# A hybrid decoder layer on one core: mixing and memory attention of tokens 0 to 511 placed among the sparse attention units of tiles 4 to 7, and the wide counts over four tiles

## The reference

```python
proj = h @ w_in[l] + b_in[l]
dq, dk, dv, iq, ik, iw, sq, sk, sv = split(proj)          # rotary on dq, dk, iq, ik, sq, sk
o_dsa = dsa_sparse_attention(dq, dk, dv, iq, ik, iw)      # 8 heads, one shared K/V head
o_swa = swa_sink_attention(sq, sk, sv, swa_sinks[l])      # 8 heads, 2 K/V heads, window 128
mix = concatenate([o_dsa, o_swa], axis=-1) @ w_o[l]
h = layer_norm(DEEPNORM_ALPHA * h + mix, ln1_g[l], ln1_b[l])
c = memory_cross_attention(h, mem, wq_mem[l], wk_mem[l], wv_mem[l], wo_mem[l])   # 4 heads, 256 tokens
h = layer_norm(DEEPNORM_ALPHA * h + c, ln2_g[l], ln2_b[l])
m = square(relu(h @ w_up[l])) @ w_down[l]
h = layer_norm(DEEPNORM_ALPHA * h + m, ln3_g[l], ln3_b[l])
```

## Time and profile before

| | |
|---|---|
| median of three runs | 1640.76 us |
| profiled execution | 1633.94 us, span 1632.1 us |
| PE busy | 1513.5 us, 93% |
| PE weight load busy | 1286.1 us, 79% |
| DVE busy | 892.2 us, 55% |
| ACT busy | 465.4 us, 29% |
| POOL busy | 536.1 us, 33% |
| chain that ended last, by engine | PE 77%, DVE 14%, ACT 3%, issue 3% |

### The profile page before, as it was taken

The page is one execution under the profiler, slowest core; times in us unless marked ns, Lnnn a source line. Parts: engine busy times, 40 slices in busy tenths (PEclk is TensorE's granted clock), DMA queues, the critical chain, the costliest instruction groups (busy, mean ns, idle before and its releaser), DMA issues.

```text
span 1632.1 us, 20732 instructions
## 1 busy us (share of the span) xinstructions
PE 1513.5 (93%) x7720; PEld 1286.1 (79%) x7720; DVE 892.2 (55%) x1819; ACT 465.4 (29%) x987; POOL 536.1 (33%) x540
## 2 busy tenths in 40 slices
PE   7999975888768999989999999999999999999996
PEld 6887754888757998768887788888888888888884
DVE  7568986778877433593426733333333333333357
ACT  3014435788674651122211201111101011111010
POOL 5232214665510003341233153333333333333300
PEclk9999997999887999999999999999999999999998
DMA  6564223554410004211110221111111110111001
GB/s 224 178 190 149 94 100 127 179 173 151 141 46 16 12 7 168 97 42 49 52 53 0 78 78 52 52 52 52 52 52 52 52 52 29 49 52 52 1 26 78
DMA packets 61331, 128.96 MB, mean 79 GB/s; under 512 B 6960, under 2 KB 34096, under 8 KB 53552
## 3 DMA queue, kind: packets, MB, share of 16 engines
q1 hardware_dynamic: 44208, 100.37, 18.6%
q10 hardware_dynamic: 17024, 27.27, 4.7%
HBM read 100.35 MB, written 27.26 MB: 78 GB/s over the span
## 4 chain that ended last, share of the span: by engine, by line
PE 77%; DVE 14%; ACT 3%; issue 3%; POOL 1%; DMA 1%; ACTq 0%; SPq 0%; DVEq 0%; POOLq 0%
PE banks L651 22%; PE banks L653 22%; PE banks L652 22%; PE banks L844 3%; PE banks L703 2%; PE banks L704 2%; DVE unread L1483 2%; PE banks L831 2%; ACT unread_wide L1047 2%; PE banks L853 1%; DVE h_buf L1792 1%; DVE bn L1778 1%; PE banks L800 1%; DVE trial L1460 1%; DVE h_buf L1801 1%
## 5 line engine op out<-in xcount | busy, mean ns | idle before, releaser
L637 POOL TENSOR_SCALAR w_hi<-raw 128x512 fp32r<-128x512 f32 x268 | 174.5, 677 | 1011.9 <-PE banks L653 685.0
L642 POOL TENSOR_TENSOR w_lo<-raw,w_hi 128x512 fp32r<-128x512 f32 x268 | 363.9, 1389 | 0.0
L1892 DVE TENSOR_TENSOR h_buf<-h_buf,banks 128x1024 f32<-128x1024 f32 x112 | 136.7, 1221 | 145.8 <-PE banks L653 145.8
L651 PE MATMUL banks<-act_hi,w_hi 128*128 128x512 f32 x512 | 200.0, 391 | 1.7 <-DVE act_lo L1771 1.7
L651 PE MATMUL banks<-w_hi,hid_hi 128*128 128x512 f32 x512 | 199.3, 389 | 1.4 <-DVE hid_lo L1872 1.4
L653 PE MATMUL banks<-act_hi,w_lo 128*128 128x512 f32 x512 | 199.9, 390 | 0.0
L652 PE MATMUL banks<-act_lo,w_hi 128*128 128x512 f32 x512 | 199.7, 390 | 0.0
L653 PE MATMUL banks<-w_hi,hid_lo 128*128 128x512 f32 x512 | 199.2, 389 | 0.0
L652 PE MATMUL banks<-w_lo,hid_hi 128*128 128x512 f32 x512 | 199.2, 389 | 0.0
L1263 ACT ACTIVATE relu_buf<-banks 128x512 f32<-128x512 f32 x64 | 38.3, 599 | 523.4 <-PE banks L653 523.4
L1867 DVE TENSOR_TENSOR relu_buf<-relu_buf 128x512 f32<-128x512 f32 x64 | 45.0, 704 | 241.9 <-ACT relu_buf L1263 241.9
(11 more groups left out here) (178 smaller groups left out, 2779.6 us busy)
## 6 DMA issues: line engine op xcount, KB each, us to landing
raw<-w_up_dram SPq DMA_DIRECT2D x16, 1024.0 KB, 4.8
raw<-w_down_dram SPq DMA_DIRECT2D x16, 1024.0 KB, 4.8
q_tile<-qk_dram SPq DMA_DIRECT2D x176, 64.0 KB, 2.1
qk_dram<-q_hi ACTq DMA_DIRECT2D x28, 256.0 KB, 2.2
qk_dram<-roped ACTq DMA_DIRECT2D x28, 256.0 KB, 2.6
x_raw<-x_t_dram SPq DMA_DIRECT2D x8, 512.0 KB, 8.4
raw<-wk_mem_dram SPq DMA_DIRECT2D x4, 1024.0 KB, 5.4
raw<-wv_mem_dram SPq DMA_DIRECT2D x4, 1024.0 KB, 5.2
```

The costliest lines, as they stand in the source:

```text
L637: pool.tensor_scalar(w_hi[s][:, col], raw[r % 2][:, col], 1.0, 1.0, ALU.mult, ALU.mult)\
L642: pool.tensor_tensor(w_lo[s][:, col], raw[r % 2][:, col], w_hi[s][:, col].bitcast(F32), ALU.subtract).then_inc(w_ready, 1)
L651: pe.matmul(dst, lh, rh, start=(first and n == 0), stop=False)
L1892: dve.tensor_tensor(h_buf[:, t, :], h_buf[:, t, :], ring_l[n % 2][:], ALU.add)\
```

## The change

- Tokens are cut into two groups of four tiles. The three stages of products are run per group: group 0 (tiles 0 to 3) with 24 products placed inside the loop of sparse units, group 1 (tiles 4 to 7) after it. `step_of_product` gives the places, counted from the first sparse step: products 0 and 1 at steps 9 and 13, then 2 to 23 at steps 19, 20, 22, 24, 26, 28, 29, 31, 33, 35, 37, 38, 40, 42, 44, 46, 47, 49, 51, 53, 54, 54. Four empty steps (`GAP`) stand between the units of tile 3 and those of tile 4.
- The 12 chunks of these stages are loaded and split twice, once for each group. Those of group 0 use slots 0 and 1 only; from `C_LATE` on four slots rotate.
- Tile 4 becomes the fourth wide tile. ACT counts 31 bits over tiles 7, 6, 5 and 4: six beside the halves 22 to 27, 21 in the band's steps 3 to 38, four at steps 1, 6, 11 and 16 of the sparse units. Each tile's trial has its own semaphore step.
- The indexer's scores move to halves 10 and 11 (tiles 2, 3) and 15 to 18 (tiles 7, 6, 5, 4). The score of each tile is prepared for the search by itself (`prepare`) in place of one block over six tiles.
- From unit 7 on POOL and not DVE makes the low parts of the rotated tiles, between its weight chunks.
- The memory tokens have a buffer of their own; they are loaded after the last index score, and split before the last half is rotated, whose rotation moves to step 2 of the band. Memory products start at step 2.

```diff
-C_G = C_MIX + 4
-C_U = C_G + 4
-C_MLP = C_U + 4
+GROUP = 4
+C_LATE = C_MIX + 12
+C_MLP = C_LATE + 12
...
+INDEX_HALVES = {10: 2, 11: 3, 15: 7, 16: 6, 17: 5, 18: 4}
+PREPARE_HALVES = {12: 2, 13: 3, 19: 7, 20: 6, 21: 5, 22: 4}
...
+WIDE_HALF = 22
+NARROW_HALVES = (13, 14)
+POOL_SPLIT = 7
...
+def unit_at(n):
+
+    d = n - NS
+    if d >= 2 * HEADS:
+        d = d - GAP if d >= 2 * HEADS + GAP else -1
+    return d if d < ND else -1
+
+
+def step_of_product(g):
+
+    if g < 2:
+        return NS + HEADS + 1 + 4 * g
+    return min(NS + 2 * HEADS + 3 + 18 * (g - 2) // 10, N_STEPS + 2)
...
+def turned_at(grp, g):
+
+    out = [(0, GROUP * grp + g + grp + 1)] if g + grp + 1 < GROUP else []
+    for gg, k in ((grp, g), (grp - 1, N_GEMM + g)):
+        if gg == grp or (grp == 1 and g < 2):
+            stage, t = divmod(k - GROUP - 2, 2 * GROUP)
+            if 0 <= stage < 3 and 0 <= t < GROUP:
+                out.append((stage + 1, GROUP * gg + t))
+    return out
...
-WIDE = N_SEL - 3
+WIDE = N_SEL - 4
...
+COUNT_TICKS = [("step", 3 + 37 * j // N_STEP_BITS) for j in range(N_STEP_BITS)]
+COUNT_TICKS += [("step", NS + n) for n in (1, 6, 11, 16)] + [("product", g) for g in range(2, WIDE_LEFT - N_STEP_BITS - 2)]
...
-    for n in range(12):
-        stage, ch = divmod(n // 2, 2)
-        last[C_MIX + n] = ("L", L_GEMM + 16 * stage + 8 * ch + NT - 1)
+    for n in range(24):
+        grp, pair = divmod(n // 2, 6)
+        last[C_MIX + n] = ("L", L_PROD[grp, GROUP * pair + GROUP - 1])
...
         def slot_of(c):
-            return c % 2 if c < C_MIX else (c - C_MIX) % 4
+            return c % 2 if c < C_LATE else (c - C_LATE + 2) % 4
...
-                if 2 <= c < C_MIX + 2:
+                if 2 <= c < C_LATE:
                     chunk_used(pool, c - 2)
-                elif C_MIX + 2 <= c < C_MIX + 4:
+                elif C_LATE <= c < C_LATE + 2:
 
                     attended(pool, 2 * NT - 1)
-                elif c >= C_MIX + 4:
+                    chunk_used(pool, C_MIX + 9)
+                elif c >= C_LATE + 2:
                     chunk_used(pool, c - 4)
...
+                for g in products_of_step(n):
+                    for key in first_turned(0) if g == 0 else ():
+                        turn(*key)
+                    product(0, g)
+            for key in first_turned(1):
+                turn(*key)
             for g in range(N_GEMM):
-                product(g)
-                if g + 2 < NT:
-                    turn_o(g + 2)
-                if transposed_at(g):
-                    turn_result(*transposed_at(g))
+                product(1, g)
...
+            for v in range(last_half):
+                if v in PREPARE_HALVES:
+                    prepare(PREPARE_HALVES[v] - FIRST_TOPK_TILE)
+                if v in NARROW_HALVES:
+                    select_for(BUDGET_BAND)
+                if wide_bit_beside_rope(v) is not None:
+
+                    pending.extend(set_wide(wide_bit_beside_rope(v)))
+                    flush(0 if v % 2 else 2)
+                rotate_and_split(v)
+                flush()
+            split_mem()
+            pending.extend(set_wide(wide_bit_beside_rope(last_half)))
+
+            for n in range(N_STEPS + 4):
...
```

More of the change, by code:

```diff
@@ L895, in product @@
                 mm.then_inc(l_full[n % 2], 1)
+                for stage, t in turned_at(grp, g):
+                    turn(stage, t)
             def up(u):
@@ L1258, in rectify @@
+            load_x(1, 0)
+            load_x(1, 1)
+            for key in first_turned(1):
+                round_turned(*key)
+            for g in range(N_GEMM):
+                gemm(1, g)
             def rectify(q):
@@ L1536, in bisect @@
                     narrow_set(*waiting)
-                def bisect_alone(c, beside):
-                    for k in range(top, -1, -1):
-                        cost, counted = narrow_tally(c)
-                        yield cost + 0.3, None
-                        more = next(beside, None)
-                        if more is not None:
-                            yield more
-                        narrow_set(c, k, counted)
-                    yield from beside
                 def finish_narrow(cols):
@@ new lines, in gemm @@
+                    if stage != 1 and ch == 1:
+                        emptied(dve, l_free, n)
+                        moments(ln_at(stage // 2, t), t)
+                turned = turned_at(grp, g) if g < N_GEMM else []
+                for key in turned:
+                    if key[0] == 0:
+                        low_turned(*key)
+                if g:
+                    stage, ch, t = parts_of_product(grp, g - 1)
+                    if stage == 1:
+                        mem_probs(grp, g - 1)
+                    elif ch == 1:
+                        norm(ln_at(stage // 2, t), t)
@@ L1864, in square @@
+            for key in first_turned(1):
+                low_turned(*key)
+            norm(ln_at(1, GROUP - 1), GROUP - 1)
+            for g in range(N_GEMM + 1):
+                gemm(1, g)
+            for g in (N_GEMM, N_GEMM + 1):
+                for key in turned_at(1, g):
+                    low_turned(*key)
             def square(q):
```

819 lines of the change are left out of this document (448 added, 371 removed).

## The result

| | kernel before | changed kernel |
|---|---|---|
| median of four runs | 1641.2 us | 1743.8 us (1735.6 to 1746.3) |
| ratio, 95% interval | | 1.061 (1.058 to 1.065) |
| span of the profiled execution | 1632.1 us | 1744.2 us |
| PE busy | 1513.5 us, 93% | 1556.5 us, 89% |
| DVE / ACT / POOL busy | 892 / 465 / 536 us | 890 / 504 / 661 us |

The change costs 102.6 us by the medians, where 41.7 were forecast.

The account below looks back on a forecast made before the run. TensorE, busy 93% of the span, was taken as the bound. The terms moved the last product from 912.4 to 954.1 us; that +41.7 on the median 1640.8 gave 1682 us, range 1640 to 1718.

Parts of the forecast that it names:

- Projections and start of the band: Up to the first memory product: projection gaps go, -7.4 us; earlier memory product, -18; less half clock there, -2.
- Band, +9 for the fourth tile: Band steps: counting tile 4 on ACT and its fourth trial on DVE add 9 us, bounds 0 and +18.
- Units 0 to 15 and the last count: Early sparse part: units, counts and products 0 and 1 end at 493.8 us; 13.5 more until product 3 at 507.3.
- Weights, +51.8: Group 0's interleaved products: with two slots, PE waits at five pair changes for POOL's rounding, 51.8 us in sum.
- Turns behind LayerNorm, +13: Interleaved part: units' transposes wait for banks DVE frees after LayerNorm, at six products, 13 us, bounds 0 and 25.
- Clock, +8: Interleaved part: half clock after five weight stalls, 2 us lost at each, and some smaller stalls: 8 us.
- rival B: Interleaved part: half clock for 17 us behind each of five stalls loses 43 us, not 8: 1717 us; chance 0.13.
- Group 1, 159 us: Last 24 products: 145 us of products and turns plus 14 of waits at the start and double turns, ending at 954.1.
- A (relief): Band and units 0 to 15: DVE freed of tile 4 lets both run at PE's pace, 1623 us; chance 0.10.
- C (counts): Band and early units: ACT's counts and DVE's selection lie more on the path, 17 us more, 1699 us; chance 0.15.

Follow-up runs that it names:

- e5: Changed kernel with tile 4's selection given back to DVE, so ACT counts three tiles: 1734.2 us, ratio 1.058.
- e1: Changed kernel with GpSimd rounding and subtracting only a quarter of the columns of group 0's weight chunks: 1696.3 us, ratio 1.035.
- e2: Changed kernel with products 4 to 23 in bursts of four, one per pair of chunks, 7 steps apart: 1676.4 us, ratio 1.023.
- e20: Changed kernel with ScalarE's square root in group 0's LayerNorms replaced by a copy: 1729.2 us, ratio 1.055.
- e16: Changed kernel with the last four counts at sparse steps 1, 3, 5 and 7 in place of 1, 6, 11 and 16: 1743.2 us, ratio 1.065.
- e11: Changed kernel with bursts of four, early turns of group 1, and last four counts at sparse steps 1, 3, 5 and 7: 1659.7 us, ratio 1.014.
- e14: Changed kernel with 18, 10, 24, 15 and 20 unused matmuls ahead of products 4, 8, 12, 16 and 20: 1737.1 us, ratio 1.062.
- e4: Changed kernel with 56, 17, 36, 22 and 30 unused matmuls ahead of products 4, 8, 12, 16 and 20: 1746.9 us, ratio 1.066.

## Why the prediction was wrong

The sign was right and so was the first mechanism; the size was 2.5 times too small. By the landmarks the last product came at 1023.4 us where 954.1 were forecast. Of these 69 us, 4 lie in the band, 1 before the first sparse mask, 16 from there to the start of product 3, 38 from there to product 23, and 10 in group 1. The medians show 61, as the two profiled executions lie further apart than the medians. By the prediction's own steps:

- **Projections and start of the band: right.** The first memory product starts 4.7 us after the last projection (5 forecast). The last band mask came at 439.7 against 435.8, and at 430.5 to 440.3 in profiles of the same program.
- **Band, +9 for the fourth tile: about right.** Taking it away gave 12 us (e5).
- **Units 0 to 15 and the last count: 67.5 us forecast from the first sparse mask to the start of product 3, 83.2 measured (444.70 to 527.85).** 13 lie ahead of the last count, which began at 511.7: product 0 with its unit took 19.9 us (469.12 to 488.97) where 10.6 were forecast, as its turn passed ACT and DVE with PE at half clock. From the last count to product 3 it was 16.1 us in place of 13.5. Early counts did not shorten A, so the lateness is DVE's and the turns' as much as ACT's.
- **Weights, +51.8: right in mechanism, 40.8 measured**, and e1 and e2 show that it is POOL's rounding and its cover; more slots for group 0 were not tried. The 15 us per pair held in three of five; the first took 21.3 and the second 16.5. The five pairs took 82 us where 77.6 were forecast, and 41 of them lay under PE's work and its other waits where 25.8 were forecast. The prediction gave 17.6 as the price beside DVE, from a LayerNorm; no pair took that, and the dear one met not a LayerNorm but DVE's finish of tiles 5 to 7. By the rule of the Trainium skill, "SBUF — State Buffer", section "Who interferes with whom", plain `tensor_scalar` passes of DVE can take the pair of ports shared with GpSimd and the form that also writes its accumulator does not; the trace agrees, 0.56 to 1.50 us and 1.15 to 1.15.
- **Turns behind LayerNorm, +13 (bounds 0 and 25): mis-sized.** The waits were 30.6 us: 21.5 on `act_lo`, and 9.1 on `prob_t`, a term that the prediction did not have at all: mixing puts LayerNorm's square roots between exponentials, and ACT loads its table ten times more (e20: 11 us of B, the clock counted).
- **Clock, +8: the step that failed most.** PE's work took 249.4 us and not 215, and 30 of these 34 us are work at half clock. Behind the five weight waits the price was right (21.8 us at half clock, 11 lost, 10 in five times the 2 us of the prediction). What was left out is that waits of 2.68 to 4.69 us for turns and probabilities went with half clock as well, in five more places. The prediction's own window from 452 to 515 us, at a mean clock of 0.73, had shown half clock among small waits, but it went into rival B and not into the sum. What came, 30 us lost, lies between the 8 of the forecast and the 43 of B, and by another way than B's: not long stretches behind five stalls but short ones behind many waits. The rule of the Trainium skill quoted with B ("TensorE: Matmul & The Clock Gate", section "HAM oscillation"), that bursts ending in a wait fall back in each round, agrees with these rows, half clock at each of the five pairs, better than with the one row at 263 us.
- **Group 1, 159 us: 169.2 measured.** No run brought it under 165, with weights, counts and order put right. PE's waits there in the changed kernel are 14.4 us on `act_lo` and 3.1 on `h_buf`, all ahead of turns of tiles: with four tiles to a stage, fewer products stand between a tile's last product and its turn. That this is the whole cause was not tested.
- **Rivals.** A (relief) is excluded: the last band mask came 4 us late and not 43 early, and with tile 4 given back to DVE (e5) the band was shorter. C (counts) has its band half right; its other half, that the late counts hold the units, was not borne out by e16.

From the start of product 3 to product 23, the 111 us over the 215 of PE work, against 72.8 forecast, are 40.8 + 21.5 + 9.1 + 5.4 of idle time and 34 of extra work, 30 of them clock. Of these 111 the order of the products alone (e2) takes away 66, and early counts (e11) 11 more. So the 103 us of the change are, by the runs in the order in which they were stacked: 63 to 67 the spacing of the products with two weight slots (with most of the 48 of e1 and some of the 11 of the table loads inside it), 4 the turns at the seam (not certain), 10 to 13 the counts' place (on the bursts alone; without them early counts gave nothing), 5 to 10 the fourth wide tile. The 13 to 17 that are left go with the cut into two groups, C's 20 us first; that it is the cut and nothing else was not isolated.

## What to carry to other kernels

Before work is interleaved, ask for each handover how much work lies in the queue between the last reader of a buffer and the first reader of its successor: bursts of four with seven units between them cost 63 to 67 us less here than the same products evenly spread. Evenly spread, every shared thing (weight slots, turned tiles' banks, ScalarE's table) changes hands at every step. In this kernel the clock had to be priced by the number of waits of a few microseconds, and not by the long ones alone.

## What the runs showed of the hardware

- A wait of 2.68 us, in work that was full of small waits, was followed by half clock (1.2 GHz) for some microseconds of product (rows of 0.63 us up to 574.68). The next such wait, 2.69 us, had half clock about it too; at 1.07 us (e20) the clock stayed full there.
- ScalarE's change between square root and exponential took 1.28 us each way on its queue; waits of PE of 2.68, 2.69 and 3.19 us went with such changes.
- Filling waits with unused matmuls regained at most 4 of some 30 us (e14), and nothing where the filler outlasted its wait (e4).
- DVE and GpSimd slowed each other both ways: 0.56 to 1.50 us for a pass over 128x768, 14.5 to 21.3 us for a pair of chunks (e16 and the changed kernel).
- The same program reached the end of the band at times 10 us apart in different profiles, with nothing changed ahead of it.
